# Merge and router of a hybrid block as one program on one Trainium2 core

## The reference, cut to what matters

```python
ya = (rms_norm(o_a, gdn_norm_g) * silu(za)) @ w_out_a          # 256 x 1024
yb = (rms_norm(o_b, gla_norm_g) * silu(rb)) @ w_out_b
y  = (gates[:, :1024] * ya + gates[:, 1024:] * yb) @ w_out     # gates = sigmoid(h @ part of w_in)
x  = x + g1 * y
h  = rms_norm(x, norm_ffn_g) * (1 + sc2) + sh2                 # written below as xn * a2 + b2
logits = h @ w_router + b_router                               # 256 x 32
top_logit, top_idx = lax.top_k(logits, 4)
top_p = softmax(top_logit)
# each token goes to 4 experts; per expert:
gu  = xb @ w_gu[e] + b_gu[e]                                   # w_gu[e] 1024 x 2048
act = min(gu[:, :1024], 7) * sigmoid(1.702 * ...) * (clip(gu[:, 1024:], -7, 7) + 1)
yb  = (act @ w_down[e] + b_down[e]) * p                        # w_down[e] 1024 x 1024
```

## Time and profile before

| | |
|---|---|
| median of 3 runs | 2254.32 us (2253.1 to 2254.37) |
| profiled execution, device time | 2256.12 us |
| its span in the trace | 2254.3 us |
| first expert weights reloaded | at 819.25 us |
| PE busy | 1987.3 us (88%) |
| DVE, ACT, POOL busy | 699.3, 498.1, 74.1 us |
| moved by DMA | 565.51 MB, 251 GB/s over the span |

### The profile page before, as it was taken

The page is one execution under the profiler, slowest core; times in us unless marked ns, Lnnn a source line. Parts: engine busy times, 40 slices in busy tenths (PEclk is TensorE's granted clock), DMA queues, the critical chain, the costliest instruction groups (busy, mean ns, idle before and its releaser), DMA issues. The chain is left out here.

```text
span 2254.3 us, 25572 instructions
## 1 busy us (share of the span) xinstructions
PE 1987.3 (88%) x9450; PEld 1091.9 (48%) x9452; DVE 699.3 (31%) x1516; ACT 498.1 (22%) x931; POOL 74.1 (3%) x67
## 2 busy tenths in 40 slices
PE   6999796989898469999999999999999697879997
PEld 3346455968786233333333333333333245547774
DVE  1475363447201522221222122212222303332323
ACT  2221721453301011111111111111111203410111
POOL 0000500100000300000000000000000000000000
PEclk8999997989999679999999999999999899889998
DMA  9452346134632469999999999999999334024342
GB/s 330 148 205 90 130 108 137 53 119 129 218 134 85 163 257 417 417 417 418 417 417 418 418 418 417 417 417 418 417 418 418 121 119 162 1 89 165 140 167 84
DMA packets 149817, 565.51 MB, mean 251 GB/s; under 512 B 35840, under 2 KB 43008, under 8 KB 111904
## 3 DMA queue, kind: packets, MB, share of 16 engines
q1 hardware_dynamic: 149760, 564.73, 64.7%
HBM read 554.67 MB, written 10.03 MB: 250 GB/s over the span
## 5 line engine op out<-in xcount | busy, mean ns | idle before, releaser
L1996 PE MATMUL expert_gb<-expert_ring,hT 128*64 128x512 f32 x1024 | 262.6, 592 | 0.0
L1996 PE MATMUL expert_lb<-expert_ring,hT 128*64 128x512 f32 x1024 | 262.5, 592 | 0.0
L2028 PE MATMUL expert_yb<-expert_ring,hT 128*64 128x512 f32 x1024 | 226.8, 595 | 11.2 <-ACT hT L1951 11.2
L1904 DVE TENSOR_SCALAR hT<-expert_gb 128x512 f32<-128x512 f32 x32 | 22.1, 692 | 551.3 <-PE expert_lb L1996 551.3
L1966 PE MATMUL expert_ob<-hT,ob 128*128 128x512 f32 x256 | 125.6, 618 | 36.8 <-DVE oa L1917 24.5
L2608 PE MATMUL ffn_pu<-ffn_hT,ffn_wu 128*128 128x256 f32 x704 | 155.7, 380 | 0.0
L2608 PEld LDWEIGHTS ffn_pu<-ffn_hT,ffn_wu 128*128 128x128 f32 x704 | 134.1, 191 | 27.2 <-issue 9.6
L440 PE MATMUL mix_in_pj<-hT,mix_in_pj_ring 128*128 128x512 f32 (+1 forms) x384 | 144.3, 535 | 1.4 <-DVE hT L551 1.4
L1996 PEld LDWEIGHTS expert_lb<-expert_ring,hT 128*64 128x64 f32 x1024 | 72.3, 137 | 147.5 <-issue 147.5
L2028 PEld LDWEIGHTS expert_yb<-expert_ring,hT 128*64 128x64 f32 x1024 | 70.6, 137 | 148.7 <-issue 128.0
L1917 DVE TENSOR_TENSOR oa<-oa,expert_ob 128x512 f32<-128x512 f32 x128 | 86.4, 685 | 174.6 <-PE expert_ob L1966 174.6
(11 more groups left out here) (466 smaller groups left out, 2398.4 us busy)
## 6 DMA issues: line engine op xcount, KB each, us to landing
expert_ring<-in_w_gu SPq DMA_DIRECT2D x256, 1024.0 KB, 11.9
expert_ring<-in_w_down SPq DMA_DIRECT2D x128, 1024.0 KB, 10.1
fill_w<-in_w_fill SPq DMA_DIRECT2D x48, 512.0 KB, 3.6
mix_in_wm<-in_w_mod SPq DMA_DIRECT2D x11, 2048.0 KB, 9.6
ffn_wu<-in_w_up_units SPq DMA_DIRECT2D x22, 1024.0 KB, 5.9
mix_in_pj_ring<-in_w_in_units SPq DMA_DIRECT2D x12, 1024.0 KB, 4.8
ffn_wd<-in_w_down SPq DMA_DIRECT2D x22, 512.0 KB, 3.4
attend_in_wi<-in_w_in SPq DMA_DIRECT2D x4, 2048.0 KB, 10.8
```

Source lines behind the costliest of these rows:

```text
L1904: v.tensor_scalar(glu, gb[:], LIMIT, None, ALU.min).then_inc(s_glu, 1)
L1996: m = pe.matmul(b[halves[h], :], xT[:, k, x], ring[:, z, c0 + 512 * h:c0 + 512 * h + 512], start=False, stop=(k == GU - 1))
L2028: m = pe.matmul(yb[halves[h], :], hidT[:, c, hh * SLOTS:(hh + 1) * SLOTS], ring[:, z, a * F + 512 * h:a * F + 512 * h + 512], start=False, ...
```

## The change

The two stages `merge_stage` and `router_stage` become one, `merge_route_stage`. The three 4 MB buffers of the merge lie in the ring's 12 units, and each group of four units is loaded with the first expert's weights when the buffer over it is used up. The split of the biases moves to POOL in `mix_in_stage`, over 128 partitions, and goes through a DRAM tensor `bias_split`. a2 and b2 are no longer applied to the transposed activations: a2 is multiplied into the router weights, and b2 makes a constant row by 8 matmuls against ones. The norm's chain runs tile by tile. The mask and the weights are built by operations over all ranks and both tiles.

```diff
 mix_in_stage:
+                sp.dma_start(bias[:], A.bias_blocks).then_inc(s_bi, 16)
                 later(4)
...
                 for f in range(F0, F1):
                     S.fill.store(sp, f)
                     S.fill.load(sp, f + 2)
-                sp.wait_ge(s_o, 96)
+                sp.wait_ge(s_bs, 7)
+                sp.dma_start(A.bias_split.rearrange("n p c -> p n c"), parts[:]).then_inc(s_o, 16)
+                sp.wait_ge(s_o, 112)
...
+            @block.gpsimd
+            def _(g):
+                link = Chain(g, s_bs)
+                g.wait_ge(s_bi, 16)
+                for n in range(3):
+                    link(g.tensor_copy(parts[:, n, :], bias[:]))
+                    if n < 2:
+                        link(g.tensor_copy(back[:], parts[:, n, :]))
+                        link(g.tensor_tensor(bias[:], bias[:], back[:], ALU.subtract))
 merge_route_stage, SP:
+                for n in range(3):
+                    sp.dma_start(S.bparts[n * NE:(n + 1) * NE]...,
+                                 A.bias_split[n]...).then_inc(s_tab, 16)
                 for f in range(F0 + 8, F1):
                     S.fill.load(sp, f)
                 sp.wait_ge(s_pa, 1)
-                sp.dma_start(w[0][:], A.w_out...).then_inc(s_wo, 16)
+                sp.dma_start(w[0], A.w_out...).then_inc(s_wo, 16)
+                sp.wait_ge(S.fill.done, F1)
+                sp.dma_start(S.pick, A.bias_pick).then_inc(s_tab, 16)
+                sp.wait_ge(s_pa, 2)
+                for n in range(8, 12):
+                    load_expert_unit(sp, A, S, 0, n)
+                sp.wait_ge(s_y, 1)
+                for n in range(4):
+                    load_expert_unit(sp, A, S, 0, n)
+                sp.wait_ge(s_t, 4)
+                for n in range(4, 8):
+                    load_expert_unit(sp, A, S, 0, n)
 POOL:
                 g.tensor_tensor(sq[:], S.oa[:], S.oa[:], ALU.mult).then_inc(s_sq, 1)
+                for b in (S.wgt, S.mask, S.pos, S.posp):
+                    g.memset(b[:], 0.0).then_inc(s_m, 1)
+                g.wait_ge(s_pa, 2)
+                g.memset(S.put[:], 0.0)
+                g.memset(S.acc, 0.0)
 ACT:
+                act.activation(warm[:], C.eps[:], ACT.Sqrt)
...
+                    act.activation(S.h2T[:, 4:8, t * P:(t + 1) * P], bank[5 + 2 * t]..., ACT.Copy).then_inc(s_xta, 1)
+                act.activation(warm[:], C.eps[:], ACT.Exp)
 PE:
                 for n, src in enumerate((S.oa, S.ob)):
                     if n == 1:
+                        pe.wait_ge(s_rt, 2)
+                        pe.wait_ge(s_wa, 1)
+                        for k in range(KT):
+                            m = pe.matmul(shift, C.ones, wrb[:, k, :], start=(k == 0), stop=(k == KT - 1))
+                        m.then_inc(s_rb, 1)
                         for f in range(F0 + 6, F1):
                             fill(f)
                         pe.wait_ge(S.fill.copied, F1)
+                        pe.wait_ge(s_br, 1)
 DVE:
+                v.wait_ge(s_rw, 32)
+                v.tensor_tensor(wrb, wr, deep(S.b2[:], NE), ALU.mult).then_inc(s_wa, 1)
...
+                v.tensor_tensor(wr, wr, deep(S.a2[:], NE), ALU.mult).then_inc(s_wa, 1)
...
+                update(0)
+                spread_of(0)
+                update(1)
+                normed(0)
+                spread_of(1)
+                normed(1)
                 for t in range(2):
                     v.wait_ge(s_tr, t + 1)
-                    for k in range(KT):
-                        v.tensor_scalar(S.h2T[:, k, t * P:(t + 1) * P], ..., S.a2[:, k:k + 1], S.b2[:, k:k + 1], ALU.mult, ALU.add)
+                    v.tensor_copy(S.h2T[:, 0:4, t * P:(t + 1) * P], bank[4 + 2 * t]...).then_inc(s_xt, 1)
...
+                route(v.tensor_tensor(one[:], iota[:]...to_broadcast([P, 2, TOPK, NE]),
+                                      idf[:, :, 0:TOPK]...to_broadcast([P, 2, TOPK, NE]), ALU.is_equal))
+                route(v.tensor_reduce(S.mask[:, :, 0:NE], one[:].rearrange("p t r n -> p t n r"), AX, ALU.add))
+                v.wait_ge(s_e, 1)
+                route(v.reciprocal(tot[:], tot[:]))
+                route(v.tensor_tensor(ex[:], ex[:], deep(tot[:], TOPK), ALU.mult))
+                route(v.tensor_tensor(one[:], one[:], ex[:]...to_broadcast([P, 2, TOPK, NE]), ALU.mult))
+                route(v.tensor_reduce(S.wgt[:, :, 0:NE], one[:].rearrange("p t r n -> p t n r"), AX, ALU.add))
```

More of the change, by code:

```diff
@@ new lines, in merge_route_stage @@
+        one = s.sb("one", [P, 2, TOPK, NE])
+        most = s.sb("most", [P, 1])
+        bank = [s.ps(f"bank{b}", [P, 2, L]) for b in range(8)]
+        (s_in, s_pz, s_wo, s_x, s_sq, s_ss, s_v, s_rt, s_sil, s_ya, s_pa, s_t, s_y, s_z, s_xs, s_n, s_rs, s_tr, s_h, s_xt, s_xta, s_ln, s_sqb) = (
+            s.sem(n) for n in ("in", "branch_gates_in", "wo_in", "x_in", "squared", "sums", "chain", "rooted", "silu", "gated",
+                               "branch", "mixed", "y_done", "out_done", "x_squares", "norm", "rstd_done", "turned", "h_done",
+                               "x_copied", "x_copied_high", "logs_done", "linear_squared"))
@@ L1606, in _ @@
                     m.then_inc(s_tr, 1)
+                for t in range(2):
+                    pe.wait_ge(s_xt, t + 1)
+                    pe.wait_ge(s_xta, t + 1)
+                    for k in range(KT):
+                        m = pe.matmul(pl[:, t, :], S.h2T[:, k, t * P:(t + 1) * P], wr[:, k, :],
+                                      start=(k == 0), stop=(k == KT - 1))
+                m.then_inc(s_l, 1)
+                pe.wait_ge(s_r, 7)
+                pe.matmul(pp[:, 0, :], tri, S.mask[:, 0, 0:NE], start=True, stop=True)
+                pe.matmul(pp[:, 1, :], C.ones, S.mask[:, 0, 0:NE], start=True, stop=False)
+                pe.matmul(pp[:, 1, :], tri, S.mask[:, 1, 0:NE], start=False, stop=True)
+                pe.matmul(pp[:, 2, :], C.ones, S.mask[:, 0, 0:NE], start=True, stop=False)
+                pe.matmul(pp[:, 2, :], C.ones, S.mask[:, 1, 0:NE], start=False, stop=True).then_inc(s_p, 1)
             @block.vector
@@ L1634, in _, with update @@
                 v.wait_ge(s_x, 16)
-                for t in range(2):
+                def update(t):
                     for h in range(2):
@@ L1785, in load_expert_unit @@
+                v.wait_ge(s_p, 1)
+                v.tensor_reduce(most[:], pp[:, 2, :], AX, ALU.max).then_inc(s_r, 1)
+                v.tensor_copy(S.pos[:, :, 0:NE], pp[:, 0:2, :])
+                v.tensor_copy(S.posp[:, :, 0:NE], pp[:, 0:2, :])
+                v.wait_ge(s_r, 12)
+                v.tensor_copy(S.count[:], most[:])
 def load_expert_unit(sp, A, S, e, n):
```

206 lines of the change are left out of this document (76 added, 130 removed).

## The result

The changed kernel takes 2220.59 us in the median of 4 runs (2219.16 to 2223.99), against 2254.32 us for three runs of the kernel before. The ratio is 0.9854, with a 95% interval of 0.9835 to 0.9874, so the changed kernel is 1.5% faster. A later comparison on another chip gave 0.9869 (0.9854 to 0.9884). A fourth run of the kernel before took 4918.06 us, more than twice the others, and is left out; what held it up is not known. The profiled execution took 2223.99 us with a span of 2222.2, 32.1 less than before.

The account below looks back on a forecast made before the run. Expert weight loading at 418 GB/s was taken as the bound, so all moves with the first reload, which hangs on the router. Terms -39.8 + 1.9 + 0 + 4.3 = -33.6 us gave 2220.7 us; range -29 to -38, 74%.

Parts of the forecast that it names:

- Norm, transposes, logits: Merge's tail, behind the last addition to x: logits end at 758.9 us, between 756.8 at full clock and 761.0 at half.
- No stage change, no biases in the way: Router: with stage change, table wait and DVE's split gone, DVE's chain starts at 758.9 us instead of 785.14.
- Mask by wide operations: DVE's router chain from logits to mask takes 2.5 us, mask at 761.4; before, the chain ran from 785.14 to 800.71.
- Count: PE's ten token-count instructions behind the mask take 1.9 us, between 1.2 and 2.3; final DVE operations add 0.9.
- Sum of the tail: Last addition to router's last operation: router ends at 764.3 us instead of 804.1, 39.8 earlier; bounds 36.9 and 42.6.
- Shift matmuls: 16 PE instructions in the merge, ahead of ten fills, add 1.9 us, or 3.5 at the logits' slower rate.
- POOL's memsets: Moved to the second branch's end, where PE waits for DVE's sum: cost 0, bounds 0 and 3.6 us.
- Loads in the merge: First expert's units loaded early: ring full by about 763 us, but issuing all at 750 would end within some 2 us.
- End of the first stage: SP's 590 KB write of the split biases, waited for at the end, costs 4.3 us; bounds 2 and 8.
- POOL's split in the first stage: Bias split on POOL early in the first stage costs 0, at most 1.5 us on PE's path.
- the hidden write: Rival: next stage gives back nearly all of the write's late start and the clock holds: -40.2 us, 2214; 10%.
- The lower clock for all of the tail: Part of a rival: 1.2 GHz throughout gives 36.9 instead of 39.8; with other upper costs -23.8 us, 2230.5; 12%.

Follow-up runs that it names:

- Experiment 8: The kernel before without the split of the expert biases, their parts cleared to zero by a POOL memset: 2238.86 us, ratio 0.993.
- Experiment 6: Changed kernel with mask and weights built again by 32 small DVE operations, one rank and tile at a time: 2233.4 us, ratio 0.9905.
- Experiments 6 to 8: Changed kernel with small mask operations (0.9905); changed kernel with a2 and b2 applied in DVE again (0.9855); kernel before without the bias split (0.993).
- experiment 5: Changed kernel with POOL clearing its two buffers by subtracting each from itself instead of memsets: one profiled execution, 2227.17 us.
- experiment 4: Changed kernel with all twelve units of the first expert loaded only after the product with w_out: 2223.65 us, ratio 0.9851.
- experiment 2: Changed kernel with the write of the split biases issued at about 200 us, ahead of the stage's last stores and fill loads: 2218.52 us, ratio 0.9831.
- experiment 3: Changed kernel with POOL's bias split waiting for DVE's scalings and the write of the split biases at 200 us: 2216.73 and 2218.26 us.
- experiment 9: Both edits (split after DVE's scalings, early write) plus unread matmuls during PE's waits: 2224.81 us; with fewer matmuls 2215.55 us, ratio 0.9823.

## Why the prediction was right, point by point

- **What bounds the kernel.** Right. The experts' stream ran at 418 GB/s before and after, and the span moved by 32.1 us where the first reload moved by 32.4.
- **Norm, transposes, logits.** Forecast: logits 9.3 us behind the last addition, between 7.2 and 11.4. Measured 8.3, with transposes mostly at 1.2 GHz and logits mostly at 2.4. The bounds were right; the middle was a hedge and not a mechanism. In six of eight traces with the changed kernel's own tail the logits were ready after 7.4 to 8.3 us, in the other two after 11.0 and 11.1. From the last addition to the first expert operation it was 15.1 to 16.0 us in the six and 18.7 and 18.9 in the two.
- **No stage change, no biases in the way.** Right. Experiment 8 puts the split alone at 14.3 to 15.4 us.
- **Mask by wide operations.** Forecast 2.5 us, measured 2.5. The comparison took 0.42, the reduction 0.58 instead of 0.36 each, and the two maxima and searches 0.75 instead of 0.95. Experiment 6 shows 8.6 us for them.
- **Count.** Forecast 1.9, measured 2.3: all at 1.2 GHz. The final four operations took 0.6 instead of 0.9.
- **Sum of the tail.** Forecast -39.8, measured 13.8 against 54.5, so -40.7; the stage change took 2.2 us instead of 2.7. The forecast's bounds add up wrongly at one end: from logits at 761.0 its own terms give 766.7 and not 767.2. By rows the 40.7 us are 11.7 for logits that start earlier, 3.2 for faster logits, 12.3 for DVE's wait behind the split, 13.1 for the chain up to the mask, and 0.4 for the rest. Experiments 6 to 8 take out the wide operations, the folding and the split. What is left, some 14 us, belongs to the merged stage, the early tables, the early loading of ACT's table, the norm tile by tile and the clock; no run separates these.
- **Shift matmuls.** Forecast +1.9, and the row took 1.87. In this pair of traces the merge up to the last addition is only 0.1 us longer, since the part in front of the shift happened to be 1.7 shorter. Over the traces it is 167.7 to 170.8 us with the shift matmuls (nine traces), and 167.6, 164.9 and 165.6 without: 2.5 us more in the mean.
- **POOL's memsets.** Forecast 0 with a bound of 3.6, measured 0; experiment 5 shows what would have cost. The row that it was taken from was weak: the maximum that kept its 0.20 us had begun before the memset (785.92 against 786.06).
- **Loads in the merge.** Forecast worth little; experiment 4 finds no difference.
- **End of the first stage.** Forecast +4.3; measured 5.2. From the issue of the write to the next stage it took 6.3 us, where 4.4 to landing and 1.0 of stage change were forecast. This term of the sum was mis-sized, inside its bounds.
- **POOL's split in the first stage.** Forecast 0, "at most one held scaling's worth on PE's path, 1.5". This step failed. I took it that DVE would be through before it mattered, and looked at its idle time behind the scalings, not at the moment when the biases land: 40.51 us, two microseconds into the scalings. DVE's scalings lost 5.9 us beside it (11.16 against 5.26), and PE needs one pair of scalings for each step: 3.0 us by the first projection's end in the mean of the traces, twice the bound. The held tensor-scalar that the prediction cites for the memsets spoke against this estimate, and I did not apply it here. The Trainium skill's rule (SBUF — State Buffer, "Who interferes with whom"), as the prediction told it, has tensor-scalars meet GpSimd in their fast mode, and the trace agrees that these meet it. Whether they were in that mode no run tests, but their length fits: 0.41 us for 256 columns from SBUF, where 128 columns from PSUM took 0.40 (the pieces of a2 and b2) and 1024 from SBUF 0.75.
- **Why the total came out.** By the two traces the span is made up like this: +4.5 us up to the last fill (forecast 0), +5.3 at the stage's end (+4.3), -1.4 over the next two stages (0), +0.1 in the merge (+1.9), -40.7 in the tail (-39.8), -0.5 at the stage change (0), and +0.5 behind it (0). Together that is -32.1, rounding apart, against -33.6. The medians moved by -33.7, since the profiled execution lies 3.4 us above the median of the changed kernel and 1.8 above that of the kernel before. So the misses stand against the tail and against spread, and an agreement of 0.1 us in the total is luck: the last fill alone started at 224.30 and 220.45 us in two traces of the same kernel.
- **The signs.** The first reload at 786.83 us (785 to 786 named), the last addition to the first reload in 28.7 us (near 30), DMA idle from 768 to 786, and 418 GB/s came as named; the token count came after 13.8 us (some 15). The second stage's start did not: 239.17 us, where 233 to 235 was named, which is the two costs of the first stage. Two operations of DVE's chain took over 0.5 us, 0.58 and 0.59.

Of the rivals, the hidden write is refuted by experiment 2. The lower clock for all of the tail was not seen, though two of the traces had it for all of the logits. The tables did not come late, and no slower stream was seen.

The best version found is the changed kernel with both edits of experiment 3, 2216.73 and 2218.26 us in two comparisons (ratios 0.9823 and 0.9825); the matmuls of experiment 9 on top made no difference that the times show.

## What to carry to other kernels

Work moved to an idle engine is free only if that engine shares nothing with one that is on the path at that moment: look up when its input lands and what the neighbour runs then. In a program of stages, whatever a stage waits for at its end should be issued earlier than the last thing nobody waits for. Where a stream bounds what follows, a prefetch is worth nothing as long as its loads, issued late, are through just when the chain asks for the next one; what counts then is that chain. A single trace prices an edit only to within what its unedited stretches move, some 4 us here: take several traces, or the times.

## What the runs showed of the hardware that was not expected

- DVE's scalings of 256 columns with two column operands were held by POOL's casts and subtractions, one by one: 5.26 us for 16 alone, 11.1 to 11.8 beside seven POOL operations of 7.7 us in all.
- A sum of two SBUF tensors and a POOL subtraction held each other in both directions, in one trace: 3.21 instead of 2.29 us on DVE, 5.65 instead of 3.60 on POOL.
- The granted clock of the same stretch differs between executions of one kernel, where PE has short waits. From the last addition to the first expert operation it is 15.1 to 18.9 us with the same instructions. The span of the profiled executions of one kernel differed by 1.4 us (2222.2 and 2220.8), its timed runs on one chip by up to 6.9.
